# Gated-delta layer of a two-layer trunk: the end of each group's mixer moves into the next group, PSUM halves alternate, and the order of conversions and mixer parts is turned round in the first ten hops

## What is computed

```python
p = x @ w_in                                  # 2048 -> q,k (2048 each), v (4096), z (4096), b, a
qkv = silu(causal_dwconv(qkv, conv_w))        # 4 taps per channel
q, k = l2_normalize(q) * 128**-0.5, l2_normalize(k)      # 16 heads, each used by two v heads
beta, g = sigmoid(b), -exp(a_log) * softplus(a + dt_bias)
o = gated_delta_rule_chunked(q, k, v, g, beta)           # 32 v heads of 128
o = o * rsqrt(mean(o*o) + 1e-6) * norm_w * silu(z)
h = o.reshape(256, 4096) @ w_out
```

## Time and profile before

| what | us |
|---|---|
| profiled execution, its own time | 3110.42 |
| its span, first to last instruction | 3108.7 |
| PE busy | 2976.7 |
| DVE busy | 1819.4 |
| ACT busy | 1436.3 |
| median of three runs | 3113.87 |

### The profile page before, as it was taken

One profiled execution on the slowest core, in us unless ns is written; L12 is line 12 of the kernel. 1 busy time (PEld: TensorE's weight loads), 2 busy tenths in 40 slices (PEclk: granted clock), 3 DMA queues, 4 the chain that ended last, 5 costly groups with the idle time before them and its releaser, 6 DMA issues.

```text
span 3108.7 us, 56912 instructions
## 1 busy us (share of the span) xinstructions
PE 2976.7 (96%) x22084; PEld 2614.8 (84%) x22084; DVE 1819.4 (59%) x2439; ACT 1436.3 (46%) x2169; POOL 13.1 (0%) x28
## 2 busy tenths in 40 slices
PE   8999999899999999999999999999998999999997
PEld 8888887688888888889888887999877888888886
DVE  4655655665555555556556656466667655555555
ACT  4544544344444434435555554446554434444442
POOL 0000000000000000000000000000000000000000
PEclk9999999999999999999999999999999999999999
DMA  7333333455555555544333333443335555555553
GB/s 227 109 110 104 110 124 132 147 217 195 188 190 192 190 192 187 193 144 136 120 107 129 130 123 129 170 142 124 115 124 196 190 188 191 193 189 193 190 189 109
DMA packets 157001, 491.94 MB, mean 158 GB/s; under 512 B 15585, under 2 KB 50529, under 8 KB 155777
## 3 DMA queue, kind: packets, MB, share of 16 engines
q1 hardware_dynamic: 154032, 476.18, 45.0%
q0 software_dynamic: 2224, 11.69, 1.0%
q10 hardware_dynamic: 544, 1.05, 0.1%
HBM read 486.76 MB, written 2.10 MB: 157 GB/s over the span
## 4 chain that ended last, share of the span: by engine, by line
PE 83%; DVE 7%; ACT 5%; issue 3%; DMA 0%; DVEq 0%; ACTq 0%; SPq 0%
PE pp L418 39%; PE mp L418 11%; PE pp L402 8%; PE mp L402 8%; PE pp L404 4%; PE mp L404 4%; ACT wh L872 1%; DVE wl L1329 1%; DVE ws L1693 1%; PE mp L800 1%; PE mp L764 1%; PE mp L748 1%; PE mp L740 1%; PE mp L806 1%; ACT ws L1188 0%
## 5 line engine op out<-in xcount | busy, mean ns | idle before, releaser
L1329 DVE TENSOR_TENSOR wl<-raw,wh 128x1024 fp32r<-128x1024 f32 (+1 forms) x936 | 1101.7, 1184 | 903.6 <-ACT wh L872 897.6
L872 ACT CAST wh<-raw 128x1024 fp32r<-128x1024 f32 (+1 forms) x936 | 944.5, 1018 | 888.5 <-PE pp L418 315.4
L418 PE MATMUL pp<-aT,wh 128*128 128x256 f32 x4704 | 907.6, 293 | 24.5 <-ACT ws L1287 13.7
L418 PEld LDWEIGHTS pp<-aT,wh 128*128 128x128 f32 x4704 | 740.5, 193 | 42.1 <-issue 24.9
L418 PE MATMUL pp<-aT,wl 128*128 128x256 f32 x2352 | 669.5, 285 | 0.0
L418 PEld LDWEIGHTS pp<-aT,wl 128*128 128x128 f32 x2352 | 454.5, 193 | 0.0
L418 PE MATMUL pp<-wh,hTh 128*128 128x512 f32 x896 | 360.9, 403 | 16.3 <-DVE hTl L1723 7.8
L402 PE MATMUL pp<-aT,wh 128*128 128x512 f32 x1024 | 363.6, 400 | 0.3 <-issue 0.3
L402 PE MATMUL mp<-aT,wh 128*128 128x512 f32 x1024 | 359.1, 396 | 0.0
L418 PE MATMUL pp<-wh,hTl 128*128 128x512 f32 x896 | 351.4, 392 | 0.0
L418 PE MATMUL pp<-wl,hTh 128*128 128x512 f32 x896 | 351.0, 392 | 0.0
(11 more groups left out here) (300 smaller groups left out, 2659.4 us busy)
## 6 DMA issues: line engine op xcount, KB each, us to landing
raw<-in_w_dram SPq DMA_DIRECT2D x800, 512.0 KB, 3.3
raw<-in_w_dram SPq DMA_DIRECT2D x136, 384.0 KB, 3.4
ws<-in_ln_dram POOLq DMA_DIRECT2D x8, 1024.0 KB, 7.7
out_dram<-xres SPq DMA_DIRECT2D x8, 256.0 KB, 2.0
ws<-in_lora_dram POOLq DMA_DIRECT2D x8, 192.0 KB, 3.5
xres<-in_x_dram ACTq DMA_DIRECT2D x2, 512.0 KB, 6.2
xres<-in_x_dram SPq DMA_DIRECT2D x2, 512.0 KB, 7.2
ws<-in_c_dram POOLq DMA_DIRECT2D x1, 576.0 KB, 7.0
```

Source lines behind the costliest of these rows:

```text
L418: last = mm(o, lhs, rhs, start=opens and m == 0, stop=end and kk == 1 and m == 2, skip_group_check=True)
L872: nc.scalar.copy(wh[:, q % RING, :, 0:width], raw[:, q, :, 0:width]).then_inc(S("hi_ready"), 1)
L1329: tt(wl[:, q % RING, :, 0:width], raw[:, q, :, 0:width], f(wh[:, q % RING, :, 0:width]), ALU.subtract).then_inc(S("lo_ready"), 1)
```

## The change

All of it is in the second layer's mixer and its stages.

1. **Ends of groups.** What a mixer did for the second part in hops 28 and 29 becomes a generator of its own (`tail1` for PE, `tail=True` for ACT and DVE), and runs beside the next stage: `along(lead, rest)` puts one part of the tail ahead of each of the next mixer's parts. ACT: `mean_square(1)` in hop 0; `out_high(1)` and then `z_out` in hop 2. DVE: `o_scale(1)` in hop 1, `out_gate(1)` (L1719) in hop 2, `out_rest(1)` (L1723) in hop 3. PE: `transpose_o(1)` in hop 2. The fifth and the eighth mixer (`whole=True`) keep their own ends. The others take `HOPS1S`, 29 hops, whose last five are (2, 1, 2, 3, 3).
2. **Buffers.** The halves of `pp` alternate through the stages, (par, 1-par, par), so that a stage starts in the half that does not hold z. The wait is that of all other panels (`lag` 2). The output projection starts in the half without z; `out1` waits for the last `hTh`, `hTl` only before unit 6 (first half) or 4 (second), where those rows come.
3. **Loops.** The hardware loops over stages are written out on all three engines.
4. **Order.** In the first ten hops (`lead_in=10`) ACT and DVE take the conversions first and the mixer's part after them.
5. **Moved and small.** `UTg` goes from DVE's hop 0 to ACT's hop 4. The four squares write to `XTc` and are not waited for one by one. DVE waits for the copy of z only in level 2 of the solve, no longer in hop 1.

```diff
+HOPS1S = HOPS1[:24] + (2, 1, 2, 3, 3)
...
     for y in range(len(hops) + wait + 1):
-        if mixer and y < len(hops):
+        held = mixer and y < len(hops)
+        if held and y >= lead_in:
             next(mixer)
         for u in range(units):
             if hop_of(2 * u, 2 * units, hops) == y and (ahead or u + LEAD < units):
                 one(u0 + u + LEAD)
+        if held and y < lead_in:
+            next(mixer)
...
+def along(lead, rest):
+
+    next(lead)
+    for _ in rest:
+        yield
+        next(lead, None)
...
+            def tail1(g):
+                yield
+                yield
+                transpose_o(g, 1, mb[0])
+                yield
...
-            def group1(n, b):
-                return blocks(n, b, "B", A, (0, 1, 0), WIDE, lag=1)
...
-            with pe.Fori(1, 5) as i:
-                drive(group1(i * 3 + P_L1, i * 3 + B_L1), 3 * UNITS, 0, mix1(i - 1), HOPS1)
...
+            def group1(n, b, par):
+                return blocks(n, b, "B", A, (par, 1 - par, par), WIDE)
...
+            for g in range(1, 4):
+                drive(group1(P_L1 + 3 * g + 3, B_L1 + 3 * g + 3, 1 - g % 2), 3 * UNITS, 0, along(tail1(g - 1), mix1(g)), HOPS1S)
...
+                def one(u, half):
+                    if u == late and half == 0:
+                        pe.wait_ge(S("mix1_out"), seen)
+                    one_(u, half)
+                return one
...
+            pe.wait_ge(S("mix1_out"), 7)
+            drive(out1(P_OUT1A, B_OUT1A, (1, 0, 1, 0), UNITS, 6, 8), 4 * UNITS, 0, along(tail1(3), mix1(4, True)), HOPS1)
...
                     for h in range(4):
-                        go(sqj, os[c][:, h, :], ACT.Square, accum_out=oss[:, h:h + 1]).then_inc(S("oss"), 1)
-                        act.wait_ge(S("oss"), 8 * g + (4 * c + h + 1))
+                        st(go(XTc[:, h, :, :].rearrange("p f c -> p (f c)"), os[c][:, h, :], ACT.Square, accum_out=oss[:, h:h + 1]))
+                    st.settle()
...
+                if tail:
+                    act.wait_ge(S("o_sum"), g1)
+                    mean_square(1)
+                    yield
+                    yield
+                    out_high(1)
+                    tail()
+                    yield
+                    return
...
+                for c in range(TT):
+                    for h in range(4):
+                        last = go(UTg[:, c, h, :], UT, ACT.Copy, scale=head(gv, c, h))
...
+                interleave(along(mix1(g - 1, g - 1, tail=z_out(P_L1 + 3 * g, g % 2)), mix1(g, g)), HOPS1S,
+                           *group1(P_L1 + 3 * g + 3, 1 - g % 2, g + 1, True), lead_in=10)
...
+                if tail:
+                    yield
+                    o_scale(1)
+                    yield
+                    out_gate(1)
+                    yield
+                    out_rest(1)
+                    yield
+                    return
...
-                for c in range(TT):
-                    for h in range(4):
-                        last = ts(UTg[:, c, h, :], UT, head(gv, c, h), None, ALU.mult)
...
-                dve.wait_ge(S("evacuated"), b + 5)
+                yield
+                dve.wait_ge(S("evacuated"), b + 4)
...
                         st.settle()
+                        dve.wait_ge(S("evacuated"), b + 5)
                         bounded(SQ, zs)
```

More of the change, by code:

```diff
@@ L851, in _ @@
[L851 to L856, removed]
+                if whole:
+                    transpose_o(g, 1, mb[0])
+                    yield
+            def group1(n, b, par):
+                return blocks(n, b, "B", A, (par, 1 - par, par), WIDE)
@@ new lines, in _, with out1 @@
+            drive(group1(P_L1, B_L1, 0), 3 * UNITS, 0, then(new_x(2), gates()), HOPS_GATES)
+            drive(group1(P_L1 + 3, B_L1 + 3, 1), 3 * UNITS, 0, mix1(0), HOPS1S)
+            for g in range(1, 4):
+                drive(group1(P_L1 + 3 * g + 3, B_L1 + 3 * g + 3, 1 - g % 2), 3 * UNITS, 0, along(tail1(g - 1), mix1(g)), HOPS1S)
+            def out1(n, b, bufs, per, late, seen):
+                one_ = blocks(n, b, "A", H, bufs, WIDE, per=per)
+                def one(u, half):
[3 more added lines that the diff above has]
+                return one
@@ L1180, in mix1 @@
                 yield
+                for c in range(TT):
+                    for h in range(4):
+                        last = go(UTg[:, c, h, :], UT, ACT.Copy, scale=head(gv, c, h))
+                        if c * 4 + h < 7:
+                            st(last)
+                last.then_inc(S("utg"), 1)
                 yield
@@ L1282, in hook, with z_out, copy @@
                         act.wait_ge(S("conv"), before * 2)
-                    nc.scalar.copy(cbuf[:, 4 * j:4 * j + 4, 3:T + 3], r2(pp[j][:, :], a=4)).then_inc(S("evacuated"), 1)
-                def z_out():
+                    nc.scalar.copy(cbuf[:, 4 * j:4 * j + 4, 3:T + 3], r2(pp[(par + j) % 2][:, :], a=4)).then_inc(S("evacuated"), 1)
+                return 3 * UNITS, wide(n), (7, 15, 23), hook, True, True, None if late else z_out(n, par)
+            def z_out(n, par):
+                def copy():
@@ L1286, in z_out @@
                     used(n, 3 * UNITS - 1)
[L1287 to L1291, removed]
+                    nc.scalar.copy(zs, r2(pp[par][:, :], a=4)).then_inc(S("evacuated"), 1)
+                return copy
+            interleave(then(new_x(2), gates()), HOPS_GATES, *group1(P_L1, 0))
@@ L1304, in _ @@
[L1304 to L1307, removed]
+            interleave(mix1(0, 0), HOPS1S, *group1(P_L1 + 3, 1, 1, True), lead_in=10)
+            for g in range(1, 4):
+                interleave(along(mix1(g - 1, g - 1, tail=z_out(P_L1 + 3 * g, g % 2)), mix1(g, g)), HOPS1S,
+                           *group1(P_L1 + 3 * g + 3, 1 - g % 2, g + 1, True), lead_in=10)
+            interleave(along(mix1(3, 3, tail=z_out(P_L1 + 12, 0)), mix1(4, 0, free=26, whole=True)), HOPS1, 4 * UNITS,
+                       wide(P_OUT1A), (), nothing, True, begun=True, lead_in=10)
@@ new lines, in _ @@
+            for g in range(1, 4):
+                interleave(along(mix1(g - 1, 0, g - 1, tail=True), mix1(g, B_L1 + 3 * g, g)), HOPS1S, *group1(P_L1 + 3 * g + 3), lead_in=10)
+            interleave(along(mix1(3, 0, 3, tail=True), mix1(4, B_L1 + 12, 0, whole=True)), HOPS1, 4 * UNITS, wide(P_OUT1A),
+                       *out_hook(P_OUT1A, B_OUT1A, (1, 0, 1, 0), UNITS, 0, True, False), True, begun=True, lead_in=10)
+            interleave(None, (), *group1(P_L1B))
+            interleave(mix1(5, B_L1B, 1), HOPS1S, *group1(P_L1B + 3), lead_in=10)
```

94 lines of the change are left out of this document (40 added, 54 removed).

## The result

The changed kernel takes 3148.7 us (median of 4 runs, 3146.5 to 3153.2), the kernel before 3114.1 beside it: ratio 1.0112, 95% interval 1.0097 to 1.0128, so 35 us slower.

A forecast was written before the change was run, and what follows sets the result against it. PE, busy 2976.7 of 3108.7 us, was taken to bound the kernel. Stage terms 7.2 + 13.2 + 6.3 + 5.2 + 9.8 - 2.7 - 1.2 gave +37.8 us on 3110.4, so 3148 us, range 3120 to 3170.

The forecast's parts named there:

- the waits at L728: PE's wait for v_act: 3.0 us per mixer instead of 0.62, in the first output stage 2.0.
- the clock: Half clock on PE behind the L704 wait: nothing to 3 us per mixer, 1.0 taken.
- The list of hops 0 to 5: ACT's and DVE's steps from a stage's start under the new order: with a tail, bounded ends at 19.6, qk_act at 30.9 us.
- The wait at L704: PE's wait for qk_act in input stages: 7.0 us with a tail, 4.4 without, where it was 0.97 or none.
- the waits for `hTl`: Output stages, PE at L418: two new waits of 5 to 6 us, before unit 6 (first) and unit 4 (last).
- the sum: All stages: 7.2 + 13.2 + 6.3 + 5.2 + 9.8 - 2.7 - 1.2 = +37.8 us.
- The gains of part 1: Ends, buffers and loops: waits for z, loop returns and slow clock behind them go, 33 us if the order cost nothing.
- The loss by the order: Hops 0 to 9: conversions waiting for PE hold back the mixer's part; L704 waits 7.0 us with a tail, 4.4 without.
- 3077: Rival (a), the order costs nothing and part 1's 33 us gain stands: 3110.4 - 33 = 3077 us; chance 0.13.
- Rival (b): Tail costs the chain nothing: 4.4 instead of 7.0 at six of eight L704, 16 us less, 3132 us; chance 0.12.
- Rival (c): Half clock behind both waits, 2 us more per mixer, or ACT's UTg products at 0.4 each: 3164 us; chance 0.11.
- the rule's fourth 1.2 us: Hardware loops: three stalls seen for four returns; by the fetch rule a fourth, about 1.2 us, would go too.

The follow-up runs named there:

- e6: Changed kernel with each mixer's end in its own stage, conversions first only on ACT in hops 3, 4 and 6: 3063.3 us.
- e1: Changed kernel with its tails, but the old order (lead_in=0) on ACT and DVE in every stage: 3108.8 us.
- e3: Changed kernel without tails, each mixer's end in its own stage, and with the old order (lead_in=0): 3092.4 us.
- e4: Kernel before with only the new order (lead_in=10) on ACT and DVE in the eight stages with a mixer: 3175.2 us.
- e9: Kernel before with only the order of e6 (conversions first on ACT in hops 3, 4, 6, never on DVE): 3103.6 us.
- e7: Changed kernel with its tails, and the order of e6 (conversions first on ACT in hops 3, 4, 6, never on DVE): 3073.2 us.
- e5: Changed kernel with the old order (lead_in=0) on DVE alone, ACT keeping the new order: 3072.9 us.
- the square: Four versions of the changed kernel: with tails, old order 3108.8 and new order 3148.7 us; without tails, old order 3092.4 and new order 3135.4 us.
- e8: Changed kernel with the eight UTg products back on DVE in hop 0: 3147.0 us.
- e11: e6 with the buffers (0, 1, 0) of the kernel before in the input stages: 3083.0 us.

## Why the prediction was right

Forecast +37.8 us; the medians moved by 34.6 and the two profiled executions by 42.8. The mechanism is the forecast's: DVE and ACT meet a cast that waits for PE ahead of a link of the chain, and `qk_act` and `v_act` come late. The terms of the chain hold one by one. Two others do not, and they cancel: the waits at L728 were put too high, the clock too low. The number owes its closeness in part to that.

**The list of hops 0 to 5.** It held to 0.2 us at almost every step: cast 4 at 3.15 (measured 3.1), gate 9.85 (9.7), z copied 11.5 (11.3), `bounded` 19.6 (19.4), `qk_act` 30.9 (31.0). The wait at L704 was put at 7.0 and is 7.4, since PE arrives at 23.6 and not 23.9; without a tail 4.4 against 4.9. In the output stages the waits for `hTl` were put at 5.1 and 5.7 and are 4.85 and 5.28, those at the transposes at 1.2 and 2.8 and are 0.51 and 1.56. All waits at L704 and for `hTl` that the sum had for the eight mixers come to 51.8 us, and those measured (L727's 41.6 and two of the three for `hTl`, 10.1) to 51.7.

**L728.** Put at 3.0 plus 1.0 of clock, it waits 0.96 to 1.86 us in the input stages; over the eight mixers the sum had 22.4 us of waiting there and 13.2 were measured. What fixes the sum of both terms is `v_act`: in all six input mixers PE starts L728's like (L751) 14.1 us after L704's (L727), whether the clock behind L704 is slow for long or not (forecast: 13.2). Its own work between the two takes 10.05 us at full clock (e6), so that wait and slow clock together are 4.0 us, as in the forecast. "The wait at L728 swallows most of it" was right, but the numbers gave the clock 1.0 and the wait 3.0, and it was the wait that got smaller: 12.2 to 13.1 us of the 14.1 PE was at work. Stages with a tail come to 109.3, 109.3, 110.9 and 109.3 us between their transposes, forecast 109.9.

**The clock.** I took 1.0 us per mixer, 8 us in all. Against it the sum also took off the slow clock of before, about 11 us by its own terms (some 2 us in each of three stages of about 105.5 against a full-clock one of 98.8 with its waits, then 1.5, 1.6 and 1.5), so by the sum PE's busy time should have been about 3 us shorter. It is 11.2 us longer at the same count of matmuls, and the time at 1.2 GHz in the layer has grown from 30.7 to 68.3 us. So the new slow stretches cost about 22 us, not 8. The waits go the other way: the sum had 74.2 us of them (51.8 and 22.4) in place of 33.3 of before, 40.9 more, and PE's idle time grew by 31.6. Clock 14 us too low and L728 9 us too high leave the traces 5.0 us above the sum. The medians are 3.2 below it; what lies between is scatter: the profiled execution is 4.5 us above its kernel's median, that of before 3.7 below. One reading of the rows was also too simple: not every stage behind a stop of 2.7 us or more reads 0.97 or 0.98, the one from 2245.50 reads 1.00 and that from 1845.28 0.99.

**The gains of part 1** were mis-sized (33 us, where they were 26.5 beside the new order and 3 beside the old), and here the reasoning failed while the number did not. "If the order cost nothing, ... 33 us" took the starts of the stages as free once PE does not wait there. In e1 and e3 the order costs nothing new, and they come out 3 and 20 us under before. ACT and DVE come out of the last mixer as late as ever (e3: ACT's first cast starts 2.5 us after PE has begun the stage), so the stop moves from the start of the stage to unit 6 and the transposes: 1.2 and 1.1 us in a stage that follows one without a mixer, 2.5 in most others. A stop in PE that a late pair of engines causes is not removed by taking away the wait; the lateness is met at the next place where PE needs them. The list for the new order was spared this error, since it started from where ACT and DVE really stand. What part 1 gives depends on the order beside it: with tails 3 us under the old order (before to e1), 26.5 under the new one (e4 to the changed kernel) and 30 under e6's (e9 to e7), where the forecast had 33 for all. The loss by the order was larger than the sum has it for the kernel before (63 us, e4), and the 26.5 of part 1 bring it back to about 37. As the time of a kernel with the old order and the rest of the change, 3077 was wrong by 32 us, and there it is `wl` that PE waits for; it takes ACT's half of the new order (e5) to come under it.

**Rival (b)**, that the tail costs the chain nothing, fell: the tail costs 13 to 16 us in the square, near the 16 it was priced at, and 9.9 between e6 and e7. **Rival (c)** fell in its time, 3164, and with e8 as far as `UTg` is concerned. Its other half, 2 us more of slow clock per mixer, is near what the clock cost (14 us more than the sum had), but since the waits at L728 shrank with it, it did not show in the time.

**The loop returns.** The section Instruction fetch mechanics of "Runtime: NRT & Kernel Launch" in the Trainium skill says that a taken branch out of the fetched window stalls for a fetch. In e4 and e9, as before, three of four returns show such a stop (0.9 to 2.3 us, each in the first microseconds of the stage), the fourth none; in all versions without loops there are none. That the fetch is the cause no run here shows. So the rule's fourth 1.2 us was rightly left out.

## What to carry to other kernels

When a schedule is written by hand for in-order engines, ask of each item not how long it takes but what it waits for, and what stands behind it. A conversion that may only start when the consumer has moved on must not stand ahead of a link of the critical chain on the second engine of the pair (DVE here, 76 us), but it belongs ahead of a link that waits for somebody anyway (ACT's sigmoid). On ACT the new order gained 36 us with tails (e1 to e5 in all ten hops, e1 to e7 in three), 29 without them (e3 to e6) and 10 in the kernel before (e9). And when a stop at a boundary is taken away, first look at whether the engines behind it are late themselves: then the stop only moves, unless the order is changed too.

## What the runs showed of the hardware

In the kernel before, six of eight stops of 2.4 to 2.9 us in dense matmul work were followed by 3.4 or 6.8 us at 1.2 GHz, and two by none (those before 2245.50 and 2347.49). In e9, which has the same eight stops, it was five, and not the same ones. So whether a slow stretch follows does not come from the stop's length alone. In both kernels the three stretches of 6.8 us are those where a second stop, that of the loop's return (0.9 to 2.3 us), comes within 3.4 us of the first; in e11 one of 6.8 follows a single stop of 2.47. With the stops of 4.4 to 7.4 us of the changed kernel and e4 it was 3.4 to 10.2 us. A second stop of about 2 us some 14 us after the first has a slow stretch of its own in four of the five input mixers of e4 where it lies between 1.8 and 2.5 us, but in the changed kernel in one of three (1.77, 1.81 and 1.86). Short stops therefore cost more than their sum: in e4 some 42 us more of waits came with 24 us more of PE's busy time.

A square of 128x128 with its sum (L1188 of the changed kernel) takes 0.29 us, and four of them 0.30 apart when the next is not made to wait for the last, against 0.43 before, so the eight squares of a mixer take about 1.0 us less; no run here separates what that alone is worth.
